# Attention as one run of 64 steps: the next head's transposes inside the steps, the values as weights in column halves

## The chip, the cores and the metric

One core of one Trainium2 chip runs the whole layer. The metric is the device time of one execution in microseconds (us).

## The reference

One layer on 1024 tokens of width 1024, all in float32: x plus the output projection of three mixers (multi-head attention, a state-space scan, a convolution), then x plus a mixture of 32 experts. The change touches the attention alone. It has 8 heads, 96 columns for a query or key (64 plain and 32 rotary), 64 for a value:

```
for i in range(L // Q_BLOCK):                       # 8 query tiles of 128 rows
    q0 = i * Q_BLOCK; kv_len = q0 + Q_BLOCK
    s = einsum('bhqd,bhkd->bhqk', q[:, :, q0:kv_len], k[:, :, :kv_len]) * scale
    mask = chunk_id[None, :kv_len] <= chunk_id[q0:kv_len, None]     # chunks of 64
    p = softmax(where(mask, s, neg), axis=-1)
    outs.append(einsum('bhqk,bhkd->bqhd', p, v[:, :, :kv_len]))
```

Tile i sees (i + 1) * 128 keys, so the 8 tiles of a head have 36 blocks of 128 by 128 between them.

## The kernel before

Every engine has its own instruction stream, written out by hand; semaphores tie them together. In time the stages are: input projection, scan and convolution (to about 297 us), attention (about 297 to 496 us), output projection and routing (to about 650 us), and a loop over the experts (to the end).

Attention is a hardware loop of four iterations, two heads in each (16 steps, `STEPS = 2 * NT`). An iteration first turns both heads: 32 transposes by TensorE (L1879) into the eight PSUM banks, which VectorE (`save_qT`, L1424) and ScalarE (`save_kT`, L924) copy to SBUF. A step is one query tile of one head, in the order 7, 0, 6, 1, 5, 2, 4, 3. On its way a tile passes:

- `scores(n)` on TensorE (L1893), two steps ahead, into banks 2*(n%2) and the next;
- `row_max(n)` on VectorE: a memset that masks half a block (L1432), then a row maximum (L1434);
- `exponentials(n)` on ScalarE (L934), which writes the exponentials and their row sums (`p_ready`);
- `turn_probs(n)` on TensorE (L1913): i + 1 transposes in "fills" of up to four, into banks 4 and 5 in turn;
- a copy of each fill to SBUF, two of three by ScalarE (L949), each third by VectorE (L1458);
- `values(n)` on TensorE (L1927), one step late: the transposed exponentials are the weights (128 columns), the head's values are streamed (64 columns), into bank 6 + n % 2, tokens on partitions;
- `save_o(n)` on VectorE: reciprocal of the row sum (L1440), and a scaled copy into `otok` (L1443).

A matmul of two float32 operands is two passes in the trace, each with its own weight load (LDWEIGHTS, in the rows as PEld); a transpose is one pass. TensorE ends each iteration with a wait on all `o_saved`. GpSimd makes the normed and rotated heads of the next iteration (L348 to L358) while one runs. In the last iteration eight "y pieces" (L911 and L916 on ScalarE, L1413 and L1416 on VectorE, 1.0 to 1.3 us each) are spread over the steps; they prepare the output projection that follows (`project_out`, L1967).

One place outside attention matters for reading the rows: the scan's input product at L1805 writes its results alternately to partitions 0 to 63 and 64 to 127 of PSUM, from weights of 64 columns:

```
for h in range(2):
    last = pe.matmul(psum[h * S:(h + 1) * S, 4 + 2 * k + r // 4, (r % 4) * P:(r % 4 + 1) * P],
                     WT[:, k, r, h * S:(h + 1) * S], U[:, 2 * r + h, :], start=True, stop=True)
```

At L1790 the weights have 32 columns, and every pass writes to the same 32 partitions.

Of the kernel before, what the change touches and what calls it, by code (L numbers as in the profile page):

```python
# [22 lines left out]
P = 128  # L23
# [13 lines left out]
def build(nc, x, positions, mix_norm, w_in, q_a_norm, w_uq, kv_a_norm, w_ukv, q_norm, k_norm,  # L37
# [34 lines left out]
    with ExitStack() as ctx:  # L72
# [7 lines left out]
        WORDS = 50300  # L80
        base = -(-nc.sbuf_base // 32) * 32
# [164 lines left out]
        bns = sb("bns", [P, NT, 8])  # L246
        psum = ctx.enter_context(nc.psum_tensor("psum", [P, 8, 512], F32))
# [24 lines left out]
        toep_in, kst_out, kpe_in, upad_ready, ssm_x_ready = sems("toep_in kst_out kpe_in upad_ready ssm_x_ready")  # L272
# [5 lines left out]
        oT_high, y_out_filled, y_out_saved, orms_out, orms_in = sems("oT_high y_out_filled y_out_saved orms_out orms_in")  # L278
        x_tail, fnorm_in, ranks_saved, wr_scaled, x2T_filled, x2T_saved = sems("x_tail fnorm_in ranks_saved wr_scaled x2T_filled x2T_saved")
        qkT_made, qT_saved, kT_saved = sems("qkT_made qT_saved kT_saved")  # L280
        s_filled, s_masked, s_max, p_ready, pT_filled = sems("s_filled s_masked s_max p_ready pT_filled")
        pT_saved_a, pT_saved_v, pv_done, sum_inv, o_saved = sems("pT_saved_a pT_saved_v pv_done sum_inv o_saved")
        o_squared, o_rms, oT_filled, oT_saved = sems("o_squared o_rms oT_filled oT_saved")
# [42 lines left out]
        FILLS = first_fill[STEPS]  # L326
        by_dve = [f % 3 == 2 for f in range(FILLS)]
# [3 lines left out]
        Y_PIECE_AT = {1: 0, 2: 1, 4: 2, 6: 3, 8: 4, 10: 5, 11: 6, 12: 7}  # L331
# [29 lines left out]
        def _(sp):  # L361
# [47 lines left out]
            sp.dma_start(kpe_d.rearrange("(p i) d -> p i d", i=NT), kst).then_inc(kst_out, 16)  # L409
            sp.wait_ge(kst_out, 16)  # L410
# [13 lines left out]
            with nc.allow_non_contiguous_dma(reason="one word per token"):  # L424
                sp.dma_start(orms_d.rearrange("(i p) a -> p (i a)", p=P), st[:, 88:88 + NT]).then_inc(orms_out, 16)
            sp.wait_ge(orms_out, 16)
# [82 lines left out]
        def _(pool):  # L509
# [95 lines left out]
            with pool.Fori(1, H // 2) as it:  # L605

                pool.wait_ge(qkT_made, 2 * it)
                for b in range(2):
                    n = [b * LINKS]
# [107 lines left out]
        def _(act):  # L717
# [200 lines left out]
            def attend(it, last_pair):  # L918
                it16, itF = act.snap(STEPS * it), act.snap(FILLS * it)
                ita, itv = act.snap(saved_a[FILLS] * it), act.snap(saved_v[FILLS] * it)  # L920

                def save_kT(b):
                    act.wait_ge(qkT_made, 2 * it + (b + 1))
                    last = act.activation(kT[b][0:QH, :].rearrange("p (k n) -> p k n", k=2), psum[0:QH, 4 * b + 2:4 * b + 4, :], ACT.Copy)  # L924
                    last.then_inc(kT_saved, 1)

                def exponentials(n):

                    act.wait_ge(s_max, it16 + (n + 1))
                    if n >= 2:  # L930
                        act.wait_ge(pT_filled, itF + first_fill[n - 1])
                    i, a = tile_of[n], am[:, n % 4, :]
                    L = (i + 1) * P
                    act.activation(prob[n % 2][:, 0:L], psum[:, 2 * (n % 2):2 * (n % 2) + 2, :].rearrange("p a n -> p (a n)")[:, 0:L],  # L934
                                   ACT.Exp, bias=a[:, 0:1], accum_out=a[:, 1:2]).then_inc(p_ready, 1)

                for b in range(2):
                    save_kT(b)
                exponentials(0)
                exponentials(1)  # L940
                for n in range(STEPS):
                    for f in range(first_fill[n], first_fill[n + 1]):
                        if not by_dve[f]:
                            act.wait_ge(pT_filled, itF + (f + 1))
                            w = min(4, tile_of[n] + 1 - 4 * (f - first_fill[n]))
                            if f >= 4:

                                act.wait_ge(pv_done, itF + (f - 3))
                            act.activation(probT[f % 4][:, 0:w, :], psum[:, 4 + f % 2, 0:w * P].rearrange("p (a n) -> p a n", n=P),  # L949
                                           ACT.Copy).then_inc(pT_saved_a, 1)  # L950
                    if n + 2 < STEPS:
                        exponentials(n + 2)
                    if last_pair and n in Y_PIECE_AT:
                        high_y_piece(Y_PIECE_AT[n])

            with act.Fori(0, H // 2 - 1) as it:
                attend(it, False)
            with act.Fori(H // 2 - 1, H // 2) as it:
                attend(it, True)
# [133 lines left out]
        def _(dve):  # L1093
# [325 lines left out]
            def attend(it, last_pair):  # L1419
                it16, itF = dve.snap(STEPS * it), dve.snap(FILLS * it)  # L1420

                def save_qT(b):
                    dve.wait_ge(qkT_made, 2 * it + (b + 1))
                    dve.tensor_copy(qT[b][0:QH, :].rearrange("p (k n) -> p k n", k=2),  # L1424
                                    psum[0:QH, 4 * b:4 * b + 2, :]).then_inc(qT_saved, 1)

                def row_max(n):
                    i = tile_of[n]
                    sv = psum[:, 2 * (n % 2):2 * (n % 2) + 2, :].rearrange("p a n -> p (a n)")
                    dve.wait_ge(s_filled, it16 + (n + 1))  # L1430

                    dve.memset(sv[0:P // 2, (i + 1) * P - P // 2:(i + 1) * P], NEG).then_inc(s_masked, 1)  # L1432
                    dve.wait_ge(s_masked, it16 + (n + 1))
                    dve.reduce_max(am[:, n % 4, 0:1], sv[:, 0:(i + 1) * P], AX, negate=True).then_inc(s_max, 1)  # L1434

                def save_o(n):

                    a = am[:, n % 4, :]
                    dve.wait_ge(p_ready, it16 + (n + 1))
                    dve.reciprocal(a[:, 2:3], a[:, 1:2]).then_inc(sum_inv, 1)  # L1440
                    dve.wait_ge(sum_inv, it16 + (n + 1))
                    dve.wait_ge(pv_done, itF + first_fill[n + 1])
                    dve.tensor_scalar(otok[:, tile_of[n], bass.ds((2 * it + n // NT) * VD, VD)],  # L1443
                                      psum[:, 6 + n % 2, 0:VD], a[:, 2:3], None, M_).then_inc(o_saved, 1)

                for b in range(2):
                    save_qT(b)
                row_max(0)
                row_max(1)
                for n in range(STEPS):  # L1450
                    for f in range(first_fill[n], first_fill[n + 1]):
                        if by_dve[f]:
                            dve.wait_ge(pT_filled, itF + (f + 1))
                            w = min(4, tile_of[n] + 1 - 4 * (f - first_fill[n]))
                            if f >= 4:

                                dve.wait_ge(pv_done, itF + (f - 3))
                            dve.tensor_copy(probT[f % 4][:, 0:w, :], psum[:, 4 + f % 2, 0:w * P].rearrange("p (a n) -> p a n", n=P)  # L1458
                                            ).then_inc(pT_saved_v, 1)
                    if n + 2 < STEPS:  # L1460
                        row_max(n + 2)
                    if n >= 1:
                        save_o(n - 1)
                    if last_pair and n - 1 in Y_PIECE_AT:
                        rest_y_piece(Y_PIECE_AT[n - 1])
                save_o(STEPS - 1)

            with dve.Fori(0, H // 2 - 1) as it:
                attend(it, False)
            with dve.Fori(H // 2 - 1, H // 2) as it:  # L1470
                attend(it, True)
# [255 lines left out]
        def _(pe):  # L1727
# [144 lines left out]
            with pe.Fori(0, H // 2) as it:  # L1872
                it16, itF = pe.snap(STEPS * it), pe.snap(FILLS * it)
                ita, itv = pe.snap(saved_a[FILLS] * it), pe.snap(saved_v[FILLS] * it)
                for b in range(2):
                    pe.wait_ge(heads_made, 2 * it + (b + 1))
# [56 lines left out]
                for n in range(STEPS):  # L1933
                    turn_probs(n)
                    if n + 2 < STEPS:
                        scores(n + 2)
# [204 lines left out]
```

## Time and profile before

| | |
|---|---|
| median of 3 runs | 1295.06 us (1293.5 to 1305.39) |
| the profiled execution | 1303.91 us, its span 1302.2 us |
| busy over the span | TensorE 90%, its loads 71%, VectorE 75%, ScalarE 55%, GpSimd 27% |
| attention, 296.7 to 496.5 us | TensorE busy 181.6 us of 199.8, VectorE 110.7, ScalarE 99.5, GpSimd 71.8 |

"Busy" counts a matmul from its start to its modelled end, so neighbours overlap; the rate of a run of matmuls is to be read from its first and last start, or from the chain of waits, where each piece has the time that it added.

### The profile page before, as it was taken

Reading aid. Unit: us, or ns where it says so; the run is one execution under the profiler, and the core shown is the slowest. Engines: PE = TensorE matmul, PEld = TensorE weight load, DVE = VectorE, ACT = ScalarE, POOL = GpSimd, SP = SyncE. Lnnn points to the kernel's source line nnn. Section 1 sums busy time; section 2 is a strip of 40 time slices with the busy share of each in tenths; the row PEclk is TensorE's granted clock in tenths of the full one; section 3 lists DMA queues with packets and bytes.
Section 4 is the critical chain, followed back from the end, with each engine's and each line's share of the span. In section 5 each row is a group of like instructions: output and inputs, shape, how many; then the busy total and the mean of one; then the engine's idle time right before and its main releaser. Section 6 shows DMA issues by size and latency. Waiting matters only on the chain.

```text
span 1302.2 us, 16421 instructions
## 1 busy us (share of the span) xinstructions
PE 1172.9 (90%) x5604; PEld 919.9 (71%) x5604; DVE 972.1 (75%) x1152; ACT 716.5 (55%) x859; POOL 356.3 (27%) x341
## 2 busy tenths in 40 slices
PE   5899989958898899999399999999999999999992
PEld 3447465646777777787378888888888887787771
DVE  1969998173555575337589999999989998898871
ACT  5511216364444464122357777777777777777750
POOL 2313014126255200011103233333323333443220
PEclk9899988688999999999589999999999999999996
DMA  6600010003000201223669999999999999999940
GB/s 202 151 1 1 1 18 9 1 1 130 1 0 0 97 1 33 82 97 122 243 279 387 366 387 387 387 401 389 384 376 372 382 365 366 371 354 367 360 134 10
DMA packets 55475, 260.80 MB, mean 200 GB/s; under 512 B 31088, under 2 KB 31760, under 8 KB 41616
## 3 DMA queue, kind: packets, MB, share of 16 engines
q1 hardware_dynamic: 45344, 243.03, 48.6%
q0 software_dynamic: 10096, 17.34, 5.5%
q8 instruction: 19, 0.31, 0.1%
q14 instruction: 16, 0.13, 0.0%
HBM read 252.25 MB, written 26.35 MB: 214 GB/s over the span
## 4 chain that ended last, share of the span: by engine, by line
PE 63%; DVE 15%; DMA 12%; ACT 3%; issue 3%; SPq 2%; POOL 0%; DVEq 0%; ACTq 0%; POOLq 0%
PE psum L2052 24%; DMA w<-in_w 10%; PE psum L2072 9%; PE psum L1967 6%; DVE arena L1301 5%; PE psum L1893 5%; PE psum L1927 4%; DVE arena L1103 3%; PE psum L1913 3%; PE psum L1745 2%; DMA out<-arena 2%; PE psum L2042 1%; PE psum L1850 1%; PE psum L1879 1%; PE psum L2058 1%
## 5 line engine op out<-in xcount | busy, mean ns | idle before, releaser
L1635 DVE TENSOR_TENSOR w_rest<-w,w_high 128x2048 fp32r<-128x2048 f32 x136 | 305.2, 2286 | 21.5 <-ACT w_high L1025 21.5
L1025 ACT ACTIVATE w_high<-w 128x2048 fp32r<-128x2048 f32 x136 | 256.4, 1913 | 87.8 <-DMA w<-in_w 52.2
L2052 PE MATMUL psum<-w_high,xgT_high 128*128 128x512 f32 x544 | 218.5, 402 | 14.0 <-DVE xgT_rest L1628 14.0
L2052 PE MATMUL psum<-w_rest,xgT_high 128*128 128x512 f32 x544 | 214.5, 394 | 0.0
L2052 PE MATMUL psum<-w_high,xgT_rest 128*128 128x512 f32 x544 | 214.1, 394 | 0.0
L1642 DVE TENSOR_TENSOR w_rest<-w,w_high 128x2048 fp32r<-128x2048 f32 x68 | 152.5, 2285 | 1.8 <-ACT w_high L1035 1.8
L1035 ACT ACTIVATE w_high<-w 128x2048 fp32r<-128x2048 f32 x68 | 126.4, 1908 | 20.8 <-DMA w<-in_w 20.6
L2052 PEld LDWEIGHTS psum<-w_high,xgT_high 128*128 128x128 f32 x544 | 103.5, 190 | 39.4 <-issue 14.8
L660 POOL DMA_INDIRECT out<-arena,idx x34 | 91.6, 2695 | 109.2 <-DVE arena L1655 106.1
L2052 PEld LDWEIGHTS psum<-w_rest,xgT_high 128*128 128x128 f32 x544 | 103.4, 190 | 22.1
L2052 PEld LDWEIGHTS psum<-w_high,xgT_rest 128*128 128x128 f32 x544 | 103.7, 191 | 20.5
L2072 PE MATMUL psum<-w_high,heT_high 128*128 128x512 f32 x272 | 109.8, 404 | 7.3 <-DVE heT_rest L1623 7.3
L2072 PE MATMUL psum<-w_high,heT_rest 128*128 128x512 f32 x272 | 107.0, 393 | 0.0
L2072 PE MATMUL psum<-w_rest,heT_high 128*128 128x512 f32 x272 | 106.9, 393 | 0.0
L1745 PE MATMUL psum<-arena 128*128 128x512 f32 x224 | 98.8, 602 | 3.0 <-ACT arena L732 3.0
L524 POOL TENSOR_SCALAR st<-st 128x1 f32<-128x1 f32 (+1 forms) x21 | 8.0, 380 | 294.1 <-ACTq L985 102.5
L934 ACT ACTIVATE arena<-psum,am 128x1024 f32<-128x1024 f32 (+3 forms) x64 | 47.3, 739 | 73.1 <-DVE am L1434 73.1
L644 POOL COPY idx<-arena 128x2 int32 (+1 forms) x34 | 32.9, 968 | 186.3 <-PE psum L2042 170.6
L1745 PEld LDWEIGHTS psum<-arena 128*128 128x128 f32 x224 | 43.1, 194 | 56.9 <-issue 56.9
L1927 PEld LDWEIGHTS psum<-arena 128*128 128x128 f32 x576 | 72.6, 192 | 9.9 <-issue 5.5
L653 POOL COPY idx<-arena 128x2 int32 (+1 forms) x35 | 39.0, 1114 | 141.1 <-DMA out<-arena,idx 120.1
L1893 PE MATMUL psum<-arena 96*128 96x512 f32 (+2 forms) x192 | 76.5, 513 | 0.0
(266 smaller groups left out, 2105.6 us busy)
## 6 DMA issues: line engine op xcount, KB each, us to landing
w<-in_w SPq DMA_DIRECT2D x102, 2048.0 KB, 18.5
arena<-in_x SPq DMA_DIRECT2D x5, 1024.0 KB, 6.2
h_scratch<-arena SPq DMA_DIRECT2D x8, 512.0 KB, 2.6
out<-arena SPq DMA_DIRECT2D x8, 512.0 KB, 3.6
arena<-in_x SPq DMA_DIRECT2D x1, 3072.0 KB, 10.0
arena<-in_w_in SPq DMA_DIRECT2D x1, 2688.0 KB, 16.2
arena<-in_w_in SPq DMA_DIRECT2D x1, 2048.0 KB, 12.2
wout_y_raw<-in_w_out SPq DMA_DIRECT2D x1, 2048.0 KB, 7.9
```

The costliest lines, as they stand in the source:

```text
L660: pool.indirect_dma_start(out=out_d, out_offset=bass.IndirectOffsetOnAxis(ap=idx[:, 2 + b, 0:1], axis=0), in_=ye[b], in_offset=None, bound ...
L1025: act.activation(w13h[k][:, c, :], w13[b][k][:, c, :], ACT.Copy).then_inc(W13H_READY[k], 1)
L1035: act.activation(w2h[:, c, :], w2s[b][:, c, :], ACT.Copy).then_inc(w2h_ready, 1)
L1301: ins = dve.scalar_tensor_tensor(cacc[:, m, :], src, dwc[:, m, k:k + 1], cacc[:, m, :], M_, A_)
L1635: dve.tensor_tensor(w13l[b][k][:, c, :], w13[b][k][:, c, :], w13h[k][:, c, :].bitcast(F32), S_).then_inc(W13_SPLIT[k], 1)
L1642: dve.tensor_tensor(w2l[b][:, c, :], w2s[b][:, c, :], w2h[:, c, :].bitcast(F32), S_).then_inc(w2_split, 1)
L1745: last = pe.matmul(bank, win[:, c, c0:c0 + P], hT[:, c, 4 * half:4 * half + 4, :].rearrange("p i j -> p (i j)"), start=(c == 0), stop=(c = ...
L1893: last = pe.matmul(psum[:, 2 * (n % 2) + k, 0:w], qT[b][0:QH, i * P:(i + 1) * P], kT[b][0:QH, 512 * k:512 * k + w], start=True, stop=True)
L1927: last = pe.matmul(psum[:, 6 + n % 2, 0:VD], probT[f % 4][:, j - j0, :], vtok[:, j, bass.ds((2 * it + n // NT) * VD, VD)], start=(j == 0), ...
L1967: last = pe.matmul(psum[:, 2 * (i % 2) + k, :], x_[:, c, i * P:(i + 1) * P], w_[:, c, 512 * k:512 * (k + 1)], start=(c == 0 and n == 0), s ...
L2052: last = pe.matmul(psum[:, k, :], x_[:, c, :], w_[:, c, :], start=(c == 0 and n == 0), stop=(c == KC - 1 and n == 2))
L2072: last = pe.matmul(psum[:, 5 + k, :], h_[:, c, :], w_[:, c, 512 * k:512 * (k + 1)], start=(c == 0 and n == 0), stop=(c == FC - 1 and n == 2))
```

## The change

- The loop and its two-head iterations go. All 64 steps (8 heads of 8) stand in one straight run with constant semaphore values, and the wait on all `o_saved` after every second head goes.
- The tiles of a head come in the order 7, 6, 1, 0, 5, 4, 3, 2, in four pairs.
- Head 0 alone is turned ahead of the steps. Every other head is turned in four parts of four transposes (keys, queries, keys, queries), in steps 1 to 4 of the head before it, all through bank 7; a part waits until the copy of the part before has been made.
- `values` becomes one block for a pair of tiles. The values are the weights (64 columns), the transposed exponentials are streamed (128 columns). The pair's first tile writes partitions 0 to 63 of bank 6, its second 64 to 127, alternately for each block of keys. The result has tokens in the free dimension, so VectorE copies it (`save_ohT`, 128x128), TensorE transposes it back one step later (`turn_values`), and `save_o` of the pair follows.
- The last pair's `turn_values` and the wait for the last `o_saved` stand behind the first `project_out`.
- GpSimd makes a head as soon as the head two before it has been turned; before, both heads of the iteration had to be.
- The y pieces keep their places in the last 16 steps. Two semaphores are merged, which changes no order.

The core of the diff (TensorE's part; "..." where lines are left out):

```diff
-        STEPS = 2 * NT
-        tile_of = [(NT - 1 - n % NT // 2) if n % 2 == 0 else n % NT // 2 for n in range(STEPS)]
+        STEPS = H * NT
+        ORDER = [i for k in range(NT // 4) for i in (NT - 1 - 2 * k, NT - 2 - 2 * k, 2 * k + 1, 2 * k)]
+        tile_of = [ORDER[n % NT] for n in range(STEPS)]
...
+        Y_PIECE_AT = {STEPS - 2 * NT + n: k for k, n in enumerate((1, 2, 4, 6, 8, 10, 11, 12))}
+        HEAD_BANK = 7
+        def next_part(n):
+            return (n // NT + 1, n % NT - 1) if n // NT + 1 < H and 1 <= n % NT <= 4 else None
...
+            def turn_head(h, part):
+                k, a = part // 2, 1 - part % 2
+                buf, turned = (qn, kn)[a][h % 2], (q_turned, k_turned)[a]
+                if part == 0:
+                    pe.wait_ge(heads_made, h + 1)
+                if h >= 1:
+                    if a == 1:
+                        pe.wait_ge(qT_saved, 2 * h + k)
+                    else:
+                        pe.wait_ge(kT_saved, 2 * h + k + 1)
+                bank = HEAD_BANK if h else 6 - 2 * a + k
+                for i in range(4 * k, 4 * k + 4):
+                    last = pe.transpose(psum[0:QH, bank, (i % 4) * P:(i % 4 + 1) * P], buf[:, i, :], ident[:, :])
...
-                            last = pe.matmul(psum[:, 6 + n % 2, 0:VD], probT[f % 4][:, j - j0, :],
-                                             vtok[:, j, bass.ds((2 * it + n // NT) * VD, VD)], start=(j == 0), stop=(j == i))
+            def values(m):
+                if m >= 1:
+                    pe.wait_ge(o_saved, 2 * m)
+                h, tiles = 2 * m // NT, tile_of[2 * m:2 * m + 2]
+                saved(first_fill[2 * m + 2] - 1)
+                for j in range(tiles[0] + 1):
+                    for k in range(2):
+                        if j <= tiles[k]:
+                            last = pe.matmul(psum[k * VD:(k + 1) * VD, 6, 0:P], vtok[:, j, h * VD:(h + 1) * VD],
+                                             probT[(first_fill[2 * m + k] + j // 4) % 4][:, j % 4, :],
+                                             start=(j == 0), stop=(j == tiles[k]))
+                last.then_inc(pv_done, 1)
+            def turn_values(m):
+                pe.wait_ge(ohT_saved, m + 1)
+                pe.transpose(psum[:, 6, P:2 * P], ohT[m % 2], ident[:, :]).then_inc(otok_filled, 1)
...
+            for n in range(STEPS):
+                turn_probs(n)
+                if n % 2 == 0 and n >= 2:
+                    turn_values(n // 2 - 1)
+                if n + 2 < STEPS:
+                    scores(n + 2)
+                if next_part(n):
+                    turn_head(*next_part(n))
+                if n % 2 == 1:
+                    values(n // 2)
...
                 project_out(i, (yTh, yTl), (wYh, wYl), y_out_filled)
+                if i == 0:
+                    turn_values(PAIRS - 1)
+                    pe.wait_ge(o_saved, H * NT)
                 turn_o(i)
```

VectorE's order within a step becomes: fill copy, `save_o` of the pair before (even steps), `row_max(n + 2)`, `save_qT` (parts 1 and 3), `save_ohT` (odd steps), y piece. ScalarE's: fill copies, `exponentials(n + 2)`, `save_kT` (parts 0 and 2), y piece.

## Rows read from the trace of the kernel before

**Rows 1.** Busy time of the engines by stretch: the four iterations of attention.

```profile
core 0: us, PE busy (x) PEld busy (x) DVE busy (x) ACT busy (x) POOL busy (x), PEclk, DMA share, GB/s
296.70:347.70 51.00, 46.64 (x296) 37.76 (x296) 25.30 (x74) 24.55 (x52) 23.01 (x26) 0.93 0.22 83
347.70:398.10 50.40, 46.16 (x297) 37.43 (x297) 25.30 (x74) 23.37 (x51) 23.02 (x26) 0.93 0.00 0
398.10:447.50 49.40, 44.95 (x297) 36.52 (x297) 25.30 (x74) 22.09 (x50) 25.80 (x34) 0.97 0.16 64
447.50:496.50 49.00, 43.89 (x297) 35.64 (x297) 34.81 (x82) 29.52 (x59) 0.00 (x0) 1.00 0.00 0
```

**Rows 2.** Chain of waits, iteration heads and a head boundary: start, us, what.

```profile
296.73 5.36 PE psum L1879 x32
302.09 1.73 PE psum L1893 x4
306.56 1.09 PE psum L1913 x8
...
347.71 3.69 PE psum L1879 x32
351.40 1.73 PE psum L1893 x4
353.35 1.24 DVE am L1434
355.87 1.97 PE psum L1913 x8
...
378.05 1.09 PE psum L1913 x8
...
382.04 1.73 PE psum L1927 x16
383.77 0.77 PE psum L1913 x7
384.55 1.29 PE psum L1893 x4
```

**Rows 3.** Groups of instructions from 290 to 497 us, all shapes of a line together.

```profile
L1434 DVE TENSOR_REDUCE am<-psum 128x1 f32<-128x1024 f32 (+3 forms) x64 | 48.5, 758 | 2.2
L934 ACT ACTIVATE arena<-psum,am 128x1024 f32<-128x1024 f32 (+3 forms) x64 | 47.3, 739 | 73.1 <-DVE am L1434 73.1
L949 ACT ACTIVATE arena<-psum 128x512 f32<-128x512 f32 x64 | 29.6, 514 | 4.9 <-PE psum L1913 4.9
L1443 DVE TENSOR_SCALAR arena<-psum,am 128x64 f32 (+1 forms) x64 | 18.2, 284 | 17.3 <-PE psum L1927 10.7 <-DVE am L1440 4.0
L934 ACT ACTIVATION_READ_ACCUMULATOR arena<-psum,am 128x1 f32 x64 | 12.4, 194 | 0.0
L1440 DVE RECIPROCAL am<-am 128x1 f32<-128x1 f32 x64 | 9.8, 154 | 0.0
L1432 DVE MEMSET psum<- 64x64 f32 x64 | 7.2, 112 | 53.7 <-PE psum L1893 53.6
L1413 DVE SCALAR_TENSOR_TENSOR wout_y_rest<-wout_y_raw,normc,wout_y_high 128x1024 fp32r<-128x1024 f32 x4 | 5.1, 1279 | 0.5 <-ACT wout_y_high L911 0.5
```

**Rows 4.** The same by shape: VectorE's copies out of PSUM, and its widest maximum.

```profile
L1458 DVE COPY arena<-psum 128x512 f32<-128x512 f32 x8 | 5.5, 687 | 1.5 <-PE psum L1913 1.4
L1458 DVE COPY arena<-psum 128x128 f32<-128x128 f32 x8 | 2.2, 281 | 0.0
```

**Rows 5.** Timeline of TensorE and its loads at L1805 (two column halves), and at L1790.

```profile
173.81 2.31 PE L1745 MATMUL psum<-arena 128*128 128x512 f32 x5
176.05 3.71 PE L1805 MATMUL psum<-arena 128*64 128x128 f32 x64
...
175.10 0.19 PEld L1745 LDWEIGHTS psum<-arena 128*128 128x128 f32 x1 [0.24 <-issue]
176.04 3.47 PEld L1805 LDWEIGHTS psum<-arena 128*64 128x64 f32 x64 [0.76 <-issue]
...
128.11 3.68 PE L1790 MATMUL psum<-arena 128*32 128x128 f32 x32
```

More of the change, by code:

```diff
@@ L246, in build @@
         bns = sb("bns", [P, NT, 8])
+        ohT = [at(OHT0 + P * b, P) for b in range(2)]
         psum = ctx.enter_context(nc.psum_tensor("psum", [P, 8, 512], F32))
@@ L326, in build @@
         FILLS = first_fill[STEPS]
+        pair_of = [n // 2 for n in range(STEPS) for _ in range(fills_of[n])]
         by_dve = [f % 3 == 2 for f in range(FILLS)]
@@ L916, in high_y_piece @@
                     act.activation(yTh[:, c, :], yTr[:, c, :], ACT.Copy).then_inc(y_part_high, 1)
[L918 to L954, printed above, removed]
@@ new lines, in _ @@
+            for k in range(2):
+                save_kT(0, k)
+            exponentials(0)
+            exponentials(1)
+            for n in range(STEPS):
+                for f in range(first_fill[n], first_fill[n + 1]):
+                    if not by_dve[f]:
+                        act.wait_ge(pT_filled, f + 1)
+                        w = min(4, tile_of[n] + 1 - 4 * (f - first_fill[n]))
+                        if f >= 4:
+                            act.wait_ge(pv_done, pair_of[f - 4] + 1)
+                        act.activation(probT[f % 4][:, 0:w, :], psum[:, 4 + f % 2, 0:w * P].rearrange("p (a n) -> p a n", n=P),
+                                       ACT.Copy).then_inc(pT_saved_a, 1)
+                if n + 2 < STEPS:
+                    exponentials(n + 2)
+                if next_part(n):
+                    h, part = next_part(n)
+                    if part % 2 == 0:
+                        save_kT(h, part // 2)
+                if n in Y_PIECE_AT:
+                    high_y_piece(Y_PIECE_AT[n])
@@ L1438, in save_o @@
+            def save_o(m):
+                for n in (2 * m, 2 * m + 1):
                     a = am[:, n % 4, :]
-                    dve.wait_ge(p_ready, it16 + (n + 1))
+                    dve.wait_ge(p_ready, n + 1)
                     dve.reciprocal(a[:, 2:3], a[:, 1:2]).then_inc(sum_inv, 1)
[L1441 to L1471, printed above, removed]
+                dve.wait_ge(otok_filled, m + 1)
+                for k in range(2):
+                    n = 2 * m + k
+                    dve.wait_ge(sum_inv, n + 1)
+                    dve.tensor_scalar(otok[:, tile_of[n], n // NT * VD:(n // NT + 1) * VD],
+                                      psum[:, 6, P + k * VD:P + (k + 1) * VD], am[:, n % 4, 2:3], None, M_).then_inc(o_saved, 1)
@@ L1474, in out_bank @@
+            save_o(PAIRS - 1)
             def out_bank(i):
@@ new lines, in scores @@
+            def scores(n):
+                h, i = n // NT, tile_of[n]
+                if n % NT == 0:
+                    pe.wait_ge(qT_saved, 2 * h + 2)
+                    pe.wait_ge(kT_saved, 2 * h + 2)
+                if n >= 2:
+                    pe.wait_ge(p_ready, n - 1)
+                L = (i + 1) * P
+                for k in range((L + 511) // 512):
+                    w = min(512, L - 512 * k)
+                    last = pe.matmul(psum[:, 2 * (n % 2) + k, 0:w], qT[h % 2][0:QH, i * P:(i + 1) * P], kT[h % 2][0:QH, 512 * k:512 * k + w],
+                                     start=True, stop=True)
+                last.then_inc(s_filled, 1)
@@ new lines, in saved, with turn_probs @@
+            def saved(f):
+                pe.wait_ge(pT_saved_a, saved_a[f + 1])
+                if saved_v[f + 1]:
+                    pe.wait_ge(pT_saved_v, saved_v[f + 1])
+            def turn_probs(n):
+                pe.wait_ge(p_ready, n + 1)
+                for f in range(first_fill[n], first_fill[n + 1]):
+                    if f >= 2:
+                        saved(f - 2)
+                    j0 = 4 * (f - first_fill[n])
+                    for j in range(j0, min(j0 + 4, tile_of[n] + 1)):
+                        last = pe.transpose(psum[:, 4 + f % 2, (j - j0) * P:(j - j0 + 1) * P], prob[n % 2][:, j * P:(j + 1) * P], ident[:, :])
+                    last.then_inc(pT_filled, 1)
@@ new lines, in turn_values @@
+            def turn_values(m):
+                pe.wait_ge(ohT_saved, m + 1)
+                pe.transpose(psum[:, 6, P:2 * P], ohT[m % 2], ident[:, :]).then_inc(otok_filled, 1)
+            for part in range(4):
+                turn_head(0, part)
+            scores(0)
+            scores(1)
+            for n in range(STEPS):
+                turn_probs(n)
+                if n % 2 == 0 and n >= 2:
+                    turn_values(n // 2 - 1)
+                if n + 2 < STEPS:
+                    scores(n + 2)
+                if next_part(n):
+                    turn_head(*next_part(n))
+                if n % 2 == 1:
+                    values(n // 2)
```

146 lines of the change are left out of this document (62 added, 84 removed).

## Prediction

> **What bounds the kernel now.** I read the windows first, one for each iteration of attention [rows 1]. The stage takes 51.0 + 50.4 + 49.4 + 49.0 = 199.8 us. TensorE is busy 44 to 47 us of each 50, VectorE 25 (35 with the y pieces), ScalarE 22 to 30, GpSimd at most 26. So TensorE sets the pace, and what is to be found is where it waits and what it spends. The reader should see that the granted clock is 0.93 in the first two iterations and 1.00 in the last: the stage loses some clock too.
>
> The chain of waits says where [rows 2]. Within an iteration the pieces of TensorE touch each other: 16 passes of values in 1.73 us (108 ns a pass), 7 transposes in 0.77 (110 ns), a score row of 6 blocks in 1.29 (0.215 us a block, two passes). At an iteration's head they do not. From 347.71 the 32 transposes take 3.69 us, the first scores end at 353.13, and the first transposes of exponentials start at 355.87: 2.7 us of standing still for mask, maximum and exponential. After that wait 8 transposes take 1.97 us and not 0.87: at the lower of the two clock levels.
>
> TensorE's work for one head is 36 blocks of scores at 0.215 = 7.7 us, 36 transposes at 0.109 = 3.9, values 72 passes at 0.108 = 7.8, 16 head transposes at 0.115 = 1.8: 21.2 us. An iteration of 50.4 us is 25.2 a head, so 4.0 us a head are waits and low clock.
>
> **Part 1, the values in two column halves.** The passes stay 72 a head, and each now streams 128 columns and not 64. What a pass costs is shown by two blocks of the same width [rows 5]. At L1790 every pass goes to the same partitions, and 32 passes take 3.68 us with the drain of the last: 0.11 us each. At L1805 they alternate between the two halves, exactly as in the new `values`: 64 passes from 176.05 to 179.76, less a drain of 0.27, is 3.44 us for 63 intervals, 0.055 us each. The two halves run beside each other. So a block of keys that both tiles of a pair see costs 4 x 0.055 = 0.219 us for both tiles, and one that only the longer sees 2 x 0.11 = 0.22. The pairs (7,6), (1,0), (5,4), (3,2) have 7 + 1 + 5 + 3 = 16 shared blocks and 4 single ones: 16 x 0.219 + 4 x 0.22 = 4.4 us a head in place of 7.8.
>
> Going from full width to halves and back, 64 times in all, has a price that the trace shows once and on one side: the last load of L1745 starts at 175.10, its pass would begin at 175.53 and end at 175.96, and L1805 begins at 176.05, 0.09 us late [rows 5]. The load that is elsewhere made ahead was here made only then (0.76 us of idle before it). From above, a full drain of one pass is 0.27 - 0.05 = 0.22 us on each side. I take 0.2 us for a pair (near the entry that was seen, twice), 0.8 a head; with the upper end it is 1.8. The Trainium skill (TensorEngine Tiling (Array Packing), Tiling Modes, Key Properties) says that changing the tiling mode drains TensorE; the one entry agrees in kind, at 0.09 us. The skill (TensorE: Matmul & The Clock Gate, Part 3) also says that a load overlaps matmuls in flight only when the row group differs. Here the row group is the same for both halves; by that rule the halves would give no gain, and the 64 loads at L1805, which lie wholly within their passes, speak against it.
>
> **Part 2, the way back.** A pair adds one transpose (0.11 us, 0.44 a head) on TensorE, and a 128x128 copy of 0.281 us on VectorE [rows 4], 1.1 us a head.
>
> **Part 3, the head's transposes inside the steps.** They cost TensorE the same 1.8 us a head. What goes is the standing still at the head of each iteration and its low clock, since scores now run two steps ahead across every head. The copies are halves of 96x512: by the 128x512 copy 0.69 us each on VectorE. A part waits for the copy of the part before through bank 7, and behind the waiting part on TensorE stands `values`.
>
> TensorE's new sum is 7.7 + 3.9 + 1.8 + 4.4 + 0.8 + 0.44 = 19.1 us a head. VectorE's is, from the groups [rows 3, 4]: maxima 6.1, memsets 0.9 (with its wait 1.2), reciprocals 1.2, scaled copies 2.3, fill copies 2.2 (now widths 512, 128, 512, 384), queries 1.4, and 1.1 new: about 15.4. ScalarE's is 5.9 + 1.6 + 3.9 + 1.2 = 12.6.
>
> **The walk.** Sums do not say what an in-order engine waits for, so I laid the three queues of one head side by side, with these durations and 0.2 us from TensorE's last start to a reader. With time 0 at the start of the scores of the next tile 7, step by step: TensorE ends those scores at 1.7, but `values` of tiles 3 and 2 waits until 3.8 for VectorE's fill copy, which stands behind the long maximum (0.3 idle). Tile 7's exponentials are ready at 4.4, before TensorE is free at 4.9: the wait at the head of the heads is gone. Tile 6's transposes wait for ScalarE's copies of tile 7, which stand behind tile 6's exponential (0.6). The first `turn_values` waits for its copy (0.2), the third head part for the copy of the second (0.3), `values` of tiles 5 and 4 for VectorE's fill copy behind the last query copy (0.6). All waits come to 2.2 us, and a head takes 21.3 us.
>
> **From start to end.** Head 0 alone is turned first: 16 transposes at the 0.168 us that they take there, 2.7 us, a copy of 0.9, scores from 300.3 and not 302.09; the first transposes at 304.8 (306.56 before) [rows 2]. Six heads of 21.3 and 1 us of low clock after that first wait give 433.6. Head 6 has four y pieces of 1.28 us on VectorE [rows 3], whose slack is 5.9 us but not where the pieces stand: each holds a fill copy or a maximum back, and I charge 1.0 for each, 25.3. Head 7 has no parts and no scores of a next head (19.1 - 1.8 - 3.2 = 14.1), waits of about 1.5 and its four pieces, charged 0.6 each: 18.0. The last values end at 476.9; before they ended at 495.8. Gain 19 us. Behind attention the first `project_out` covers the last copy (0.6 us saved), and the wait ahead of `turn_o` costs about as much. ScalarE's eight squares of `otok` start some 6 us later against TensorE; the results are needed 50 us later, and the bank hand-over has a buffer of two tiles, so I cost it at nothing; if that cover were gone it would be at most 6 us. GpSimd needs 11.5 us a head and has more than a head's time. The rest of the kernel only moves forward, as its loads follow TensorE's progress.
>
> On the profiled execution's scale this is 1303.9 - 19 = 1285; that execution was 9 us above the median, so on the median's it is 1295 - 19 = 1276. A difference of 1% (13 us) is about what a measurement of this kernel can tell.
>
> **The rivals.** (A) The halves do not overlap when they accumulate: L1805 has no accumulation over blocks, only over its two passes. Then values take 72 x 0.108 + 0.8 + waits; TensorE's sum is 22.6, some of the 2.2 us of waits is covered, a head takes about 23.6, and the gain over seven heads is 16 us less: 3 to 6 us, 1290. Against it: the two passes of one matmul at L1805 do accumulate, in turn with the other half. (B) Slower: the change of mode drains and refills at more than the entry showed. It decides at 0.4 us a change: 0.6 us more a pair than I took, on 32 pairs, is 19 us, the whole gain. At 0.6 us a change it is 32 us more, a quarter of which falls into waits that are there anyway: 1295 - 19 + 24 = 1300, and up to 1308 with none covered. Against it stands the one entry at 0.09. (C) The waits of the walk cost more: each is an in-order queue with two steps of lookahead, and if they were 3.5 us a head and not 2.2, the gain would be 9 us, 1286. (D) They cost nothing, and the y pieces hide: 19.1 a head and 14 + 1 for the last give a gain of 36 us, 1259.
>
> **How the numbers follow.** The forecast (gain of 13 to 30 us) has 0.62; A 0.12; B 0.06; C 0.12; D 0.08. The likeliest stands at 1276. The range takes in D and reaches to A and C, and leaves out B: 1259 to 1293. Faster by over 1%: the forecast and D, and a part of C, 0.73. Within 1%: most of C, and A, 0.21. Slower: B, 0.06.
>
> **What would show it.** In the profile after: 72 passes of values a head at 55 ns a start in the shared blocks; a stage of about 180 us; the granted clock at 1.00 from the second head on; VectorE busy some 15 us of each 21; no wait for the exponential of tile 7, but short ones for ScalarE's and VectorE's fill copies; and the stages behind with their lengths unchanged. What would make it wrong: passes at 108 ns (A), loads of the values that start only after the last full-width pass has drained and long gaps there (B), or idle time before `values` and `turn_values` that grows with the step (C).

## The result, and the profile after

The changed kernel takes 1286.2 us (median of 8 runs, 1283.99 to 1290.84), the kernel before 1296.71 us (1293.5 to 1310.05). The ratio is 0.9898, with a 95% interval of 0.9865 to 0.9931: by this ratio 13 us less, between 9 and 17.5; the two medians lie 10.5 us apart. The profiled execution has a span of 1284.7 us against 1302.2. Attention, from the first transposes of a head to the first matmul of `project_out`, takes 480.34 - 296.56 = 183.8 us; before it was 496.47 - 296.73 = 199.7 [rows 2]. Its end in the kernel before, and in the kernel after:

```profile
496.47 0.49 PE L1967 MATMUL psum<-wout_y_high,yT_high 128*128 128x512 f32 x1 [0.66 <-DVE arena L1443]
...
480.34 0.50 PE L1989 MATMUL psum<-wout_y_high,yT_high 128*128 128x512 f32 x1
```

These 16 us lie inside the interval of the whole, and what follows attention takes 804.4 us and took 805.7. They may still be too many for a typical execution: the profiled one of the kernel before took 1303.91 us, 7 above the median of 1296.71. In all eleven profiles of this study everything outside attention takes 1098 to 1103 us, so that about 192 to 197 us are left for attention in a median execution of the kernel before (an estimate), and not 199.7.

The windows of the kernel after, one for each head (columns as in [rows 1]):

```profile
core 0: us, PE busy (x) PEld busy (x) DVE busy (x) ACT busy (x) POOL busy (x), PEclk, DMA share, GB/s
306.00:327.20 21.20, 19.81 (x152) 13.64 (x150) 12.73 (x37) 10.81 (x26) 13.98 (x17) 1.00 0.13 51
...
391.60:413.00 21.40, 20.14 (x154) 13.91 (x153) 13.63 (x43) 10.93 (x26) 11.48 (x14) 1.00 0.01 2
413.00:434.50 21.50, 20.23 (x154) 14.01 (x153) 13.73 (x43) 10.94 (x26) 6.79 (x13) 1.00 0.38 147
434.50:459.90 25.40, 22.00 (x164) 15.05 (x163) 18.75 (x49) 16.25 (x33) 0.00 (x0) 1.00 0.01 2
459.90:480.40 20.50, 13.76 (x118) 9.73 (x118) 14.18 (x40) 10.90 (x24) 0.00 (x0) 1.00 0.00 1
```

The granted clock is 1.00 in all the steps, from the first head to the last, where it was 0.93, 0.93 and 0.97 in the first three iterations [rows 1]. (Ahead of the steps, from 296.5 to 306, it is 0.81.) From one tile 7 to the next a head takes 21.46 us, five times over; before, two heads took 49.3 to 50.4. But the last two windows stand out: TensorE is busy 13.8 us of the last 20.5, and VectorE 18.8 of the 25.4 before. Those are the heads with the y pieces.

The chain of waits of the kernel after over one whole head (start, us, what):

```profile
370.15 1.02 PE psum L1928 x8
371.28 0.43 PE psum L1910 x2
371.90 0.99 PE psum L1928 x7
373.12 0.44 PE psum L1896 x4
373.55 1.90 PE psum L1940 x30
375.45 0.37 PE psum L1928 x2
375.84 0.33 PE psum L1948
376.17 1.30 PE psum L1910 x4
377.97 0.59 issue
378.56 0.69 DVE arena L1427
379.29 0.64 PE psum L1896 x4
379.94 0.58 PE psum L1940 x6
...
383.81 0.61 DVE arena L1468
384.55 1.50 PE psum L1940 x22
386.05 0.59 PE psum L1928 x4
386.76 1.74 PE psum L1910 x4
388.75 1.11 issue
389.86 0.56 DVE arena L1468
390.55 1.06 PE psum L1940 x14
391.61 1.02 PE psum L1928 x8
```

L1940 is `values` of a pair, L1928 `turn_probs`, L1948 `turn_values`, L1910 the scores, L1896 a head part, L1427 and L1468 VectorE's copies of queries and of fills. Tile 7's transposes (x8) follow at once on `values` at 391.61: the 2.7 us ahead of them are gone. The four blocks of values take 1.90, 0.58, 1.50 and 1.06 us, 5.04 a head, against 7.8 before. And at three places in a head it is not TensorE that the chain runs through but VectorE's copies: of queries (378.56), of tile 4's fill (383.81, behind another copy of queries at 383.13), of tile 2's fill (389.86).

### The profile page after: what moved, and what is told of

Same layout as the page of the kernel before. It is cut to its first block, busy times and chain, and to the rows that moved or that the text cites. A ratio compares the mean times of both kernels' runs of the same rounds, so it can differ in the third digit from the quotient of the medians.

```text
span 1284.7 us, 16070 instructions
## 1 busy us (share of the span) xinstructions
PE 1152.7 (90%) x5636; PEld 882.2 (69%) x5636; DVE 979.3 (76%) x1192; ACT 713.7 (56%) x865; POOL 351.3 (27%) x341
## 4 chain that ended last, share of the span: by engine, by line
PE 62%; DVE 17%; DMA 10%; issue 4%; ACT 4%; SPq 2%; POOL 0%; DVEq 0%; ACTq 0%; POOLq 0%
PE psum L2077 25%; PE psum L2097 10%; DMA w<-in_w 8%; PE psum L1989 6%; DVE arena L1307 5%; DVE arena L1109 3%; PE psum L1940 3%; PE psum L1910 3%; PE psum L1756 2%; PE psum L1928 2%; PE psum L2067 2%; DMA out<-arena 2%; PE psum L1861 1%; PE psum L2083 1%; PE psum L1859 1%
## 5 line engine op out<-in xcount | busy, mean ns | idle before, releaser
L2077 PEld LDWEIGHTS psum<-w_high,xgT_high 128*128 128x128 f32 x544 | 103.1, 189 | 38.3 <-issue 13.8
L2077 PEld LDWEIGHTS psum<-w_rest,xgT_high 128*128 128x128 f32 x544 | 102.9, 189 | 22.4
L655 POOL COPY idx<-arena 128x2 int32 (+1 forms) x34 | 32.4, 954 | 182.6 <-PE psum L2067 167.8
L1756 PEld LDWEIGHTS psum<-arena 128*128 128x128 f32 x224 | 43.0, 193 | 56.6 <-issue 56.6
L1910 PE MATMUL psum<-arena 96*128 96x512 f32 (+1 forms) x192 | 72.5, 487 | 0.8 <-DVE arena L1427 0.8
L664 POOL COPY idx<-arena 128x2 int32 (+1 forms) x35 | 33.0, 943 | 144.2 <-DMA out<-arena,idx 123.7
L1307 DVE SCALAR_TENSOR_TENSOR arena<-arena,dwc 128x1024 f32<-128x1024 f32 x58 | 69.4, 1273 | 0.0
```

What stands on the lines that cost most here:

```text
L1307: ins = dve.scalar_tensor_tensor(cacc[:, m, :], src, dwc[:, m, k:k + 1], cacc[:, m, :], M_, A_)
L1756: last = pe.matmul(bank, win[:, c, c0:c0 + P], hT[:, c, 4 * half:4 * half + 4, :].rearrange("p i j -> p (i j)"), start=(c == 0), stop=(c = ...
L1910: last = pe.matmul(psum[:, 2 * (n % 2) + k, 0:w], qT[h % 2][0:QH, i * P:(i + 1) * P], kT[h % 2][0:QH, 512 * k:512 * k + w], start=True, st ...
L2077: last = pe.matmul(psum[:, k, :], x_[:, c, :], w_[:, c, :], start=(c == 0 and n == 0), stop=(c == KC - 1 and n == 2))
```

## The experiments

All runs start from the changed kernel. "Stage" is measured as above; "head" is the time from the transposes of one tile 7 to those of the next, in the heads without y pieces.

For the kernel before, the last two heads come from its chain of waits, with the end at 496.47 (the rows ahead of 455.64 are used at the end):

```profile
327.62 1.09 PE psum L1913 x8
...
398.07 3.69 PE psum L1879 x32
...
406.23 1.74 PE psum L1913 x8
...
427.48 1.09 PE psum L1913 x8
...
447.48 3.69 PE psum L1879 x32
...
455.64 1.09 PE psum L1913 x8
...
475.81 1.09 PE psum L1913 x8
```

| kernel | stage us | head us | last two heads us | ratio to before, 95% interval |
|---|---|---|---|---|
| before | 199.7 | | 20.2 + 20.7 | 1 |
| after | 183.8 | 21.46 | 23.5 + 22.4 | 0.9898, 0.9865 to 0.9931 |
| halves in turn | 203.1 | 23.53 | 25.6 + 25.9 | 1.0015, 0.9985 to 1.0045 |
| old values | 210.1 | 23.58 | 25.7 + 32.4 | 1.0078, 1.0046 to 1.011 |
| old values, y spread | 197.7 | 23.58 | 23.6 + 22.0 | 0.9992, 0.9959 to 1.0025 |
| old tile order, y spread | 204.7 | 24.45 | 24.6 + 21.2 | 1.0042, 1.0015 to 1.0069 |
| stop each second head | 191.1 | 21.43, 23.52 | 23.5 + 23.7 | 0.9932, 0.99 to 0.9964 |
| y pieces spread | 177.2 | 21.46 | 21.5 + 17.8 | 0.9838, 0.9779 to 0.9897 |
| fills first | 181.6 | 21.19 | 23.5 + 22.1 | 0.987, 0.9812 to 0.9928 |
| both | 175.7 | 21.20 | 21.7 + 17.9 | 0.9805, 0.9761 to 0.9849 |
| first fill moved | 174.0 | 20.85 | 21.4 + 17.6 | 0.9798, 0.9755 to 0.9841 |

**Do the halves run beside each other?** The same passes, without alternation:

```diff
-                for j in range(tiles[0] + 1):
-                    for k in range(2):
+                for k in range(2):
+                    for j in range(tiles[0] + 1):
```

> The changed kernel with one edit: the values of a pair's first tile all come first, then those of its second, so that the two column halves are never used in alternation; instructions, shapes and waits stay. Theory (the halves run beside each other only when they alternate, and TensorE is the bound): a pass costs 0.11 us, values 72 x 0.11 + 0.6 = 8.5 us a head and not 5.0; of these 3.5 us about 1.2 fall into waits that are there anyway, so a head takes 23.8 us and not 21.5, the stage about 200 us and not 183.9, the whole 16 to 18 us more than the changed kernel, level with the kernel before. Rival (VectorE's and ScalarE's queues bound the steps, the gain came from the head boundaries alone): the stage grows by less than 5 us.

Measured: 1304.75 us, stage 203.1, head 23.53. The chain of this run at the values of tiles 7 and 6, 5 and 4, 3 and 2:

```profile
377.77 3.08 PE psum L1940 x30
...
389.95 2.21 PE psum L1940 x22
...
396.67 1.33 PE psum L1940 x14
```

30 passes take 3.08 us, where they took 1.90: 0.103 us a pass instead of 0.063. It is the same number of the same instructions, so the alternation, and nothing else of the new form, makes the gain of the passes. The stage grew by 19 us, and the whole gain of the change is gone. The rival's 5 us is out. The theory's 3.5 us a head for the passes was too much: the four blocks take 7.2 us, 2.2 more, and a head 2.07 more. The passes do start 0.109 us apart, but where the first tile's end and the second's begin the halves still meet: seven starts in a row, from 379.10 to 379.49, are 0.055 us apart on average. Eight heads at 2.07 make 16.6 of the 19 us; the rest lies in the start (0.6), the first head (0.7) and the last, where the granted clock is 0.93.

**What is the new form worth against the old one?** Exponentials as weights again, one tile of a pair after the other, in the pairs and the one run of the changed kernel (not shown: `save_o` waits for `values` and no longer for `turn_values`, and the last `turn_values` goes too):

```diff
-  last = pe.matmul(psum[k * VD:(k + 1) * VD, 6, 0:P], vtok[:, j, h * VD:(h + 1) * VD], probT[...][:, j % 4, :], ...)
+  last = pe.matmul(psum[:, 6, P + k * VD:P + (k + 1) * VD], probT[...][:, j % 4, :], vtok[:, j, h * VD:(h + 1) * VD], ...)
-                    turn_values(n // 2 - 1)
-                    save_ohT(n // 2)
```

> The changed kernel with the old form of the values: exponentials as weights, 64 value columns streamed, no copy of the transposed result and no transpose back; pairs, order, one run and head parts stay. Theory: values cost 72 x 0.108 = 7.8 us a head against 5.0 + 0.4 for the way back, 2.4 more on TensorE; VectorE loses 1.2 us and the wait for the copy goes, so a head takes 1.3 to 2 us more, the stage 193 to 198 us: the one run is worth 2 to 7 us by itself, the column halves the rest. Rival (the one run gave all, the column halves are a wash because of the way back): the stage stays within 3 us of 183.9.

Measured: 1312.86 us, stage 210.1. The theory's 193 to 198 us missed. A head does take 2.1 us more (23.58), but the last one took 32.4 us. Windows of this run, an earlier head and the last:

```profile
421.60:445.20 23.60, 22.40 (x150) 17.23 (x150) 12.43 (x38) 11.00 (x27) 5.39 (x13) 1.00 0.34 134
470.90:503.20 32.30, 26.96 (x126) 22.59 (x125) 14.94 (x39) 12.23 (x27) 0.00 (x0) 0.67 0.01 2
```

The granted clock of the last head is 0.67; the values of tiles 7 and 6 took 6.42 us in it (475.54 to 481.96), after TensorE had stood still for 1.8 us behind a fill copy. So I ran the same kernel without the y pieces in its last heads:

> The run with the old form of the values, with the y pieces spread as well. Its last head took 32.3 us at the lower clock level for much of it, which hid what the one run is worth with the old values. Theory (the clock fell because TensorE stood still for 1.5 to 1.8 us several times in a head that has y pieces): the clock stays at 1.00, heads take 23.6 us to the last but one and the last about 20.5, the stage about 193 us: 7 us less than the 199.7 of the kernel before, so one run with pairs gives 7 and the column halves the other 16. Rival (the old values in pairs lower the clock by themselves): the last head stays above 28 us.

Measured: 1300.67 us, stage 197.7, last head 22.0, the others 23.58. The granted clock of the last head is 0.88, not 1.00 as the theory had it and not 0.67: most of the low clock went with the y pieces, a part is there without them, and what lowers it stays open. That one run is worth 7 us with the old values is wrong: against the profiled execution before it is worth 2. The column halves are worth the rest: with the y pieces spread in both, 197.7 - 177.2 = 20.5 us, of which 2.12 a head, 17 in all, at a granted clock of 1.00; most of what is left lies in the first head and in the last, at 0.88.

**What is a stop worth?** At heads 2, 4 and 6 the first two scores are issued only after the last values of the head before (likewise `row_max` and `exponentials`):

```diff
-                if n + 2 < STEPS:
+                if n + 2 < STEPS and n % 16 < 14:
                     scores(n + 2)
...
+                if n % 16 == 15 and n + 2 < STEPS:
+                    scores(n + 1)
+                    scores(n + 2)
```

> The changed kernel, but at heads 2, 4 and 6 no scores run ahead over the boundary: the first two scores of the head are issued after the last values of the head before, on all engines alike. This brings back the three inner stops of the old loop. Theory: each costs scores, maximum and exponential standing alone (about 2.7 us), and the granted clock falls after it as it did in the kernel before (1 us): 10 to 12 us for the three, stage 194 to 196 us. Rival (the steps have slack that a stop only uses up): under 4 us, and the clock stays at 1.00.

Measured: 1294.5 us, stage 191.1. The three heads with a stop took 23.52 us, the others 21.43: 2.1 us a stop, 6.3 for three, plus 1 at the end. This is between the two expectations. The clock stayed at 1.00 over the stops, so that half of the theory fell: these stops do not bring the low level back. The 1 us at the end is not theirs: in the last head, without a stop, the granted clock is 0.93, and the values of tiles 5 and 4 take 2.79 us and not 1.50. TensorE's idle row at the first stop (the other two show the same 1.24):

```profile
349.69 1.09 PE L1934 MATMUL psum<-ident,arena 128*128 128x128 f32 x8 [1.24 <-ACT arena L941]
```

The old loop's stops show 2.53 us there. Its second tile is tile 0, with 2 passes of scores; here it is tile 6, with 4 long ones that fill part of the wait. So this run prices a stop in the new order of tiles, without 32 transposes in a row; the old stops may have cost more, which was not tried.

**Does the order of the tiles matter?**

```diff
-        ORDER = [i for k in range(NT // 4) for i in (NT - 1 - 2 * k, NT - 2 - 2 * k, 2 * k + 1, 2 * k)]
+        ORDER = [(NT - 1 - n // 2) if n % 2 == 0 else n // 2 for n in range(NT)]
```

> The kernel with the y pieces spread, but with the tile order of the kernel before, so the pairs are (7,0), (6,1), (5,2), (4,3): only 1 + 2 + 3 + 4 = 10 blocks of keys are shared and 16 are single, against 16 and 4. Theory (a shared block costs 0.219 us for both tiles, a single one 0.22 for one): values cost 26 x 0.22 + 0.6 = 6.3 us a head and not 5.0, a head takes 22.3 to 22.8 us and not 21.46, the stage is 184 to 188 us and not 177.2. Rival (a long tile behind a short one hides its maximum and exponential better, which the kernel before shows between its stops, so that the waits fall by as much): a head stays within 0.4 us of 21.46.

Measured: 1305.21 us, stage 204.7, head 24.45: more than the theory gave. The chain of this run at the values of (5,2), (4,3), (7,0) and (6,1):

```profile
371.38 1.50 PE psum L1941 x18
...
377.60 1.28 PE psum L1941 x18
...
383.18 1.93 PE psum L1941 x18
...
389.90 1.67 PE psum L1941 x18
```

All have 18 passes. With 0.055 us for a shared pass and 0.11 for a single one they would take 1.32, 1.10, 1.76 and 1.54: what is left is 0.18, 0.18, 0.17 and 0.13 us. The first three blocks follow a wait, and what is left there is the end of their last pass: it lasts 0.27 us, and the chain counts it whole and not the 0.11 to a next start. Only the fourth follows at once on other work; its 0.13 us is the change into halves. The changed kernel has the same at its two blocks that follow at once (1.90 - 1.76 and 0.58 - 0.44: 0.14 each). The change back stands in the row behind each block. Two transposes behind the values of tiles 7 and 6, in the changed kernel and in the run with old values:

```profile
375.45 0.37 PE psum L1928 x2
...
381.21 0.22 PE psum L1926 x2
```

That is 0.15 us; four transposes take 0.59 and 0.44, eight 1.02 and 0.88. So the two changes cost 0.29 us together, and the first of them costs nothing where a wait stands ahead of the block. The values cost 1.3 us a head more than with 16 shared blocks, as expected; the other 1.7 us are mostly waits for fill copies and query copies, which the short tiles no longer cover: TensorE is idle 0.5 to 1.5 us at four places in a head, where in the changed kernel the longest such gap is 0.6.

**Why are the last two heads long?** Four of the pieces went to one a head (on ScalarE in heads 0 to 3, on VectorE in heads 1 to 4) and four into the last 20 steps, on VectorE ahead of `save_ohT`:

```diff
-        Y_PIECE_AT = {STEPS - 2 * NT + n: k for k, n in enumerate((1, 2, 4, 6, 8, 10, 11, 12))}
+        Y_PIECE_AT = {n: k for k, n in enumerate((5, 13, 21, 29, 45, 49, 53, 57))}
+        Y_REST_AT = {n: k for k, n in enumerate((9, 17, 25, 33, 49, 53, 57, 61))}
...
+                if n in Y_REST_AT:
+                    rest_y_piece(Y_REST_AT[n])
                 if n % 2 == 1:
                     save_ohT(n // 2)
```

> The changed kernel with the eight y pieces taken out of the last 16 steps: one in each of heads 0 to 3, four in the last 20 steps, on VectorE just ahead of its copy of the transposed result in steps 1 and 5 of a head, where it waits for values. Theory (the pieces stand in front of fill copies and maxima, which is why the last two heads take 25.4 and 22.4 us): heads 0 to 5 keep 21.5 us, head 6 falls to about 22, head 7 to about 18.5, the stage to about 177 us, 7 us less in all. Rival (the last heads are long because TensorE waits for something else, such as the low lookahead at the end): the stage stays within 2 us of 183.9.

Measured: 1281.72 us, stage 177.2, as the theory said; the last two heads took 21.5 and 17.8. Windows of this run for these two:

```profile
433.80:455.30 21.50, 20.24 (x153) 13.95 (x152) 15.83 (x45) 12.74 (x28) 0.00 (x0) 1.00 0.01 2
455.30:473.10 17.80, 15.14 (x129) 10.96 (x128) 12.25 (x39) 9.74 (x23) 0.00 (x0) 1.00 0.00 1
```

A piece of 1.25 us is free where VectorE waits for `values` anyway: the heads that have one take 21.45 or 21.46 us like the rest.

**Can the waits of the steps be had?** Two edits: the last query copy of a head one step later, and the fill of tile 2 by ScalarE ahead of tile 7's exponential.

```diff
-        by_dve = [f % 3 == 2 for f in range(FILLS)]
+        by_dve = [f % 12 in (2, 5, 8) for f in range(FILLS)]
...
+                if next_part(n - 1) and next_part(n - 1)[1] == 3:
+                    save_qT(next_part(n - 1)[0], 1)
...
+                if n % NT != 7:
+                    save_fills(n)
+                if n % NT == 6:
+                    save_fills(n + 1)
```

> The changed kernel with two edits in the queues that the walk names: VectorE copies the last quarter of the next head's queries one step later, behind the fill copy that values of tiles 5 and 4 wait for; and the fill of tile 2 is copied by ScalarE ahead of tile 7's exponential, and no longer by VectorE behind tile 7's maximum. Theory (TensorE waits 0.4 to 0.6 us at each of these two places in every head): a head takes 20.5 to 20.8 us and not 21.46, the stage about 177 us, 6 to 7 us less. Rival (the waits only move on to the next copy in the queue): under 2 us.

Measured: 1284.82 us, stage 181.6, head 21.19. Only 0.27 us a head: nearer to the rival. The chain of this run at the places of 383.81 and 389.86 above:

```profile
382.46 0.19 ACT arena L941
382.65 0.18 ACT arena L956
...
382.92 1.49 PE psum L1946 x22
```

(L1946 is `values` in this kernel.) This is where the second wait went. The values of tiles 5 and 4 no longer follow VectorE's copy of 0.61 us, but ScalarE's of tile 4's second fill, which stands behind tile 3's exponential. Tile 2's copy is off the chain altogether: `values` of tiles 3 and 2 follow at once on the scores.

> The edits of the runs with the y pieces spread and with the two fill copies moved, together. Theory: they act on different stretches (the last two heads; every head), so the gains add: stage 183.8 - 6.6 - 6.5, about 171 us, 12 to 14 us less than the changed kernel. Rival (both use up the same slack of VectorE): no better than the better of the two, about 177 us.

Measured: 1276.78 us, stage 175.7: less than the sum. Spreading gave 6.6 us alone, the moved copies 2.2, together 8.1.

The last run takes the combined one and moves two more fills:

```diff
-        by_dve = [f % 12 in (2, 5, 8) for f in range(FILLS)]
+        by_dve = [f % 12 in (0, 2, 5, 8) for f in range(FILLS)]
...
-                if n % NT != 7:
+                if n % NT not in (1, 7):
                     save_fills(n)
-                if n % NT == 6:
+                if n % NT in (0, 6):
                     save_fills(n + 1)
```

> The combined run, with one more wait of the walk attacked: VectorE and not ScalarE copies tile 7's first fill, and ScalarE copies tile 6's second fill ahead of the exponential of tile 1. Theory (0.5 to 0.6 us a head are lost because ScalarE's copies of tile 7 stand behind tile 6's exponential): another 3 to 5 us, stage about 167 us. Rival (VectorE, with 0.7 us more a head, becomes what values and the scaled copies wait for): within 1 us of the combined run, or slower.

Measured: 1275.25 us, stage 174.0, head 20.85: 0.35 us a head, 1.7 for the stage, half of what was expected. (From its first tile 7 on, this run gains 2.7 us; its start, ahead of the steps, took 0.95 longer than the combined run's.) This is the fastest profile of the study, with a ratio of 0.9798 (0.9755 to 0.9841) to the kernel before. Its median is 1.5 us below the combined run's, which these runs cannot tell apart.

## Why the prediction was right, and where it was off

Forecast was a gain of 19 us. In attention, between two profiled executions, it is 16; on the whole kernel 13 by the ratio (9 to 17.5), and 10.5 between the medians. So the median of 1286.2 us lies in the range of 1259 to 1293, which was wide, but 10 us above the likeliest 1276, at the lower edge of the forecast's own gain of 13 to 30 us. It is even the 1286 that was given to rival C: the number alone could not have told the two apart, the rows do.

- **Part 1, a pass at 0.055 us in shared blocks and 0.11 in single ones, 0.2 us a pair for the mode.** The passes are right: the single starts are 0.109 us apart for two in a shared block and for one in a single one. L1805 [rows 5] was the right row to price them by. The change of mode was priced too low for a pair, 0.2 us against 0.29 measured (0.14 in, 0.15 out): the one entry at L1805 shows only the first late start. But two of the four entries of a head lie in waits, so that a head pays about 0.9 us, near the 0.8 in the sum. The rule of the Trainium skill (TensorEngine Tiling (Array Packing), Tiling Modes, Key Properties) that a change of mode drains agrees with these 0.14 and 0.15 us. Its other rule (TensorE: Matmul & The Clock Gate, Part 3), that a load overlaps matmuls in flight only when the row group differs, is not borne out: the halves have one row group, and alternating them took 1.2 us off 30 passes.
- **The walk, 21.3 us a head with 2.2 us of waits.** Right: 21.46, and at the places that it named. (The waits that it lists add up to 2.0. TensorE's idle gaps in a head are 1.3 us, and each of the five also lays open the end of the pass before it, 0.16 us that otherwise overlaps: about 2.) VectorE's sum was too high, 15.4 against 13.7 busy. The walk had the waits' size and not their depth: behind each copy it named stands another at nearly the same time, so taking two away gave 0.27 us a head and not 0.8.
- **Six heads at 21.3 and 1 us of low clock.** Right: the first transposes of tile 7 of head 6 start at 434.46, forecast 433.6. That they meet is in part luck: the clock did not fall, and the 1 us went instead into the start. The first transposes of exponentials came at 305.72, forecast 304.8, as the 16 transposes of head 0 took 3.66 us, at a granted clock of 0.50, and not 2.7.
- **Heads 6 and 7.** This is the term that was mis-sized. Forecast 25.3 + 18.0 = 43.3 us, measured 45.9 (23.5 + 22.4). The sum for the eight pieces was right, 6.4 us charged and 6.6 measured (by the run that spread them), though it falls otherwise: 2.0 in head 6 and 4.6 in head 7. What was wrong is head 7 without them, 15.6 us forecast, where the spread run took 17.8 with two pieces on VectorE and one on ScalarE, in covered places. I scaled the waits with the work, to 1.5 us, but with no scores of a next head TensorE has nothing to do while it waits: it was busy only 15.1 us of 17.8.
- **Behind attention.** Costed at nothing: 804.4 us and 805.7 before, right.
- **The rivals.** A (halves do not overlap) has now a price: 2.07 us a head, where I gave it 2.3; over eight heads, and with the low clock that came at the end, 19 us, the whole gain, where I had counted 16. B (drain) decided at 0.4 us a change and is 0.14 to 0.15. C would have shown as longer heads and did not. D (waits that cost nothing, hidden y pieces) failed on both: the heads kept their waits, and the pieces cost 6.6 us.

Where did the old kernel's time go, then? Six heads took 149.1 us before from tile 7 to tile 7 (306.56 to 455.64) and take 128.7 now: 20.3 us less. The last two took 40.8 and take 45.9: 5 us given back. With the y pieces spread the two take 39.3. The old steps had hidden the pieces nearly all: from the second tile 7 of an iteration to the iteration's end took 20.1, 20.0 and 20.0 us without pieces, and 20.7 in the last iteration, with five of VectorE's eight. The start gives 0.7.

Three prices are known by themselves. The low clock cost the old loop about 4 us (an estimate): from the first tile 7 of an iteration to the second took 21.06, 22.18 and 21.25 us, and 20.17 in the fourth iteration, at a granted clock of 1.00, though three pieces stand in it. The stops are worth 6.3 us at full clock in the new tile order, the halves 19 to 20. These come to about 30, and with the y pieces spread the whole change gained 22.5 us. So something in the new form costs: with the old values it takes 23.58 us a head, though the stops are gone. The pairs are the suspect, as they make `values` wait for the copies of two tiles; this is argued and not shown. The passes of the old form are not slower in pairs: their single starts are 0.112 us apart in the old loop and in the run with old values alike. A single run with the old values step by step would settle it; it was not tried, since the head parts now hold the bank that its double buffer needs.

## What to carry to other kernels

When a matmul's output has 64 rows or fewer, price its passes by a block of the same trace that alternates column halves, and count how many pass pairs can truly alternate: the overlap is had almost only there, and here the old order of the tiles cost 3.0 us a head, 1.3 in the values and the rest mostly in waits. Lay the in-order queues side by side before believing a sum of busy times, above all in the last round, where work that used to fill the waits is missing. And when steps are merged, look again at every small job that was tucked between them: moving eight pieces to where their engine waits anyway gave 6.6 us, four tenths of what the whole change had given in attention.

## What was not expected of the hardware

- The granted clock stayed at 1.00 over three stops with 1.2 us of idle TensorE each, where it had fallen after the old loop's stop of 2.5 us in three iterations (and not in the fourth); and it fell to 0.67 in the last head of the run with old values, which cost 6.5 us beyond the 25.9 that the halves-in-turn run took for the same head, at 0.93. With the same instructions spread otherwise, the same head took 22.0, at 0.88. The last head of the changed kernel has idle gaps of up to 1.8 us too and kept 1.00. What decides between them is open.
- The two halves need not alternate pass by pass to overlap: in the halves-in-turn run seven starts in a row are 0.055 us apart where one half ends and the other begins, against 0.109 elsewhere.
- Passes with exponentials as weights (128 columns, 64 streamed) start 0.112 us apart, those with values as weights (64 columns, 128 streamed) 0.109 without alternation: streaming twice as much costs no more here.
